# Tables instead of two constant paces for the work beside the RWKV heads

## The chip, the cores and the metric

One core of a Trainium2 chip runs the whole program. The metric is the device time of one execution, in microseconds (us); lower is better. The core's engines run their own instruction streams: PE is TensorE (PEld its weight loads), DVE is VectorE, ACT is ScalarE, POOL is GpSimd, SP is SyncE, which starts the weight transfers.

## The reference, cut to what matters

The program computes three transformer blocks, one after the other. Only the first is touched, and in it two branches that read the same normed input of 528 rows:

```python
o_rwkv = rwkv7_mix(p_rwkv, ...) @ rwkv_w_o[layer]
o_diff = diff_attention(p_diff, ...) @ diff_w_o[layer]
...
def step(S, inp):
    rt, wt, kt, vt, at, bt = inp
    sa = jnp.einsum('bhvk,bhk->bhv', S, at)
    S = S * wt[:, :, None, :] + sa[..., None] * bt[:, :, None, :] + vt[..., None] * kt[:, :, None, :]
    y = jnp.einsum('bhvk,bhk->bhv', S, rt)
    return S, y
```

`rwkv7_mix` has 16 heads of 64 columns, `diff_attention` 8 pairs of heads (causal softmax of two score matrices, their difference times V). Neither needs the other until both are done.

## The kernel before, in words

There is no scheduler: for each engine a Python function writes the instructions in their final order, and each instruction waits for semaphores of the others. In the first block the three functions are `pe_rwkv` (L872), `act_rwkv` (L1133) and `dve_rwkv` (L1269). Each loops over 8 heads here called head 0 to head 7 (each is two RWKV heads, `hh` 0 and 1). The recurrence is computed in 6 chunks of 88 rows (`NCH`, `CH`). One pass of the loop has these parts:

1. transposes of V, At, B and Kh to rows (`rw_tr`), then the products of keys and queries within the chunks (`rw_gram`: ATp, ATo, Ak, Mb, Mk). DVE masks Ak, Mb and Mk, four instructions each (`rw_masked`), and prepares the first inverse (`rw_x`, `rw_xt`, `rw_mask`). Then AV;
2. the inverse of a triangular matrix by doubling: levels 2, 4, 8 and 16, each a product Y and a product Z with small 32x32 matmuls, then 32 and 64 with other shapes;
3. W (`rw_w2`, copied out by ACT as `rw_wt`) and U0 (`rw_u`, copied out by DVE as `rw_u0`);
4. the chain over the chunks, in which chunk ci waits for chunk ci-1: PE multiplies the state by W (`rw_ws`), DVE adds it to U (`rw_us`), PE forms the step of the state (`rw_ds`), DVE adds it to the state (`rw_s`); beside it PE forms the output (`rw_yc`).

Between the parts the function calls `advance()` (L314), at 41 places a head, the same 41 on each engine. They are called place 0 to place 40 here: 0 to 3 in the transposes, 4 to 11 in the products and masks, 12 to 19 in the levels up to 16, 20 to 23 in levels 32 and 64, 24 to 40 in the chain (24 ahead of chunk 0's step of the state, 25 behind it, 26 behind its output, 27 behind `rw_ws` of chunk 1). At a place two kinds of other work may be written into the stream, each cut into steps by `yield`:

- **the work queue** `self.work`: for places 0 to 11 the finish of the head before (`finish`: norm, bonus and output gate), 5 steps; from place 12 on the preparation of the next head (`prep`), 16 steps. On PE its steps 1 to 12 are twelve groups of 12 matmuls of 128x264 (the projections of r, k and v, weights in half slabs), step 13 the matmuls of the decay and of a. On ACT and DVE steps 4, 8 and 12 copy a projection out (`rw_sh`) and mix it with its shifted self (`rw_mixed`, two instructions of DVE of 128x528); step 13 is two sigmoids and three exponentials of ACT and the scan of DVE (`rw_cum`); steps 14, 15 and 16 are DVE's three, four or five wide instructions each, ending with `rw_khat`, for which PE waits ahead of the next head's transposes.
- **the generator** `self.beside` (`pe_diff` L1467, `act_diff` L1566, `dve_diff` L1633): differential attention, 30 steps for each of its 8 heads. Steps 1 to 12 are the projections of q, k and v (on PE 12 matmuls of 128x264 each); 13 transposes V; then for five blocks of queries come the scores (steps 14, 16, 19, 22, 25), on DVE the maximum in the same step and the softmax weights one step later, on PE the transposes of the weights (17, 20, 23, 26, 28) and the product with V (18, 21, 24, 27, 29); step 30 is the norm. The last block's scores (step 25) take four PSUM banks at once.

`advance()` takes one step of the queue, and of the generator 0.7 steps on average:

```python
    def advance(self):

        self.due += self.pace
        while self.due >= 1:
            self.due -= 1
            next(self.beside, None)
        while self.work:
            try:
                next(self.work[0])
                return
            except StopIteration:
                self.work.pop(0)
```

So a head takes 28.7 steps of attention, and which step stands at which place moves from head to head. The preparation of head 0 is written ahead of the loop by `drain()` (L332), with 11 steps of attention beside it at the same pace. Behind the loop, four gate projections (`gate`, L1107) and the finish of head 7 follow, with what is left of the attention.

PSUM has 8 banks, taken in turn (`bank`); whoever takes a bank waits for the instruction that last emptied it. DVE and ACT work strictly in the written order, and a wait of theirs holds up all that stands behind it.

## Time and profile before

| | |
|---|---|
| median of 3 runs | 3495.51 us (3495.16 to 3499.75) |
| profiled execution: its own time, its span | 3494.43 us, 3492.6 us |
| the 8 heads (from the first transpose to the last output) | 107.1 to 1019.2 us of the span |
| PE, DVE, ACT, POOL busy over the span | 88%, 47%, 35%, 24% |
| granted TensorE clock, mean | 0.915 of full speed |

The times of the trace count from the start of the span. In a timeline row the bracket tells how long the engine had been idle before the row and what ended the idle time. TensorE's clock has two levels in the rows, 1.00 (2.4 GHz) and 0.50 (1.2 GHz); a mean between them is a mix over the stretch.

### The profile page before, as it was taken

The page shows a single profiled execution, that of the slowest core. Times are in us where ns is not written, and L with a number is a line of the kernel's source. Part 1 is how long each engine was busy: PE and PEld are TensorE (multiplying, and loading weights), DVE is VectorE, ACT ScalarE, POOL GpSimd, SP SyncE. Part 2 cuts the span into 40 slices and gives each one's busy share as a digit, 9 for nine tenths or more (in the row PEclk, how much of TensorE's full clock was granted, in tenths as well). Part 3 has the DMA queues.
Part 4 walks back from the last instruction along what each step waited for, and adds up shares of the span by engine and source line. Part 5 has one row for each costly group of instructions (what it writes and reads, how often), then busy time and mean ns, then how long its engine had stood idle before and what let it go on. Part 6 is the DMA issues. An engine that isn't in the chain of part 4 may idle for free.

```text
span 3492.6 us, 58593 instructions
## 1 busy us (share of the span) xinstructions
PE 3090.8 (88%) x24118; PEld 2488.9 (71%) x24118; DVE 1644.7 (47%) x2885; ACT 1220.7 (35%) x2083; POOL 831.1 (24%) x808
## 2 busy tenths in 40 slices
PE   6888898889898999999888788888889999888887
PEld 6767787778677878886677566666669998545565
DVE  3544544565524344342454364555565556432432
ACT  2323433433322243233433343433244343332341
POOL 4122121112112100001445355441000002513332
PEclk9888999989869999999899899999999999878998
DMA  3101111111004233331212122214325556301111
GB/s 122 29 28 35 29 41 30 31 32 41 29 25 164 84 121 94 93 97 52 61 55 64 43 64 65 60 58 142 91 78 174 164 164 181 119 20 46 43 46 60
DMA packets 94811, 259.79 MB, mean 74 GB/s; under 512 B 10672, under 2 KB 10672, under 8 KB 93264
## 3 DMA queue, kind: packets, MB, share of 16 engines
q1 hardware_dynamic: 81968, 209.11, 20.3%
q0 software_dynamic: 7680, 35.40, 3.0%
q10 hardware_dynamic: 4896, 11.54, 0.9%
q8 instruction: 191, 3.13, 0.4%
q14 instruction: 76, 0.62, 0.1%
HBM read 236.08 MB, written 19.92 MB: 73 GB/s over the span
## 4 chain that ended last, share of the span: by engine, by line
PE 72%; DVE 13%; ACT 10%; issue 3%; DMA 2%; POOL 1%; ACTq 0%; DVEq 0%; SPq 0%; POOLq 0%
PE psum L430 70%; DVE arena L362 6%; ACT arena L347 5%; ACT arena L355 3%; DVE arena L371 3%; PE psum L434 2%; ACT L343 1%; DMA ring<-in_w 1%; DVE arena L366 1%; ACT L347 1%; DVE arena L383 1%; POOL arena L362 1%; DVE arena L393 0%; DVE arena L386 0%; DMA arena<-in_x 0%
## 5 line engine op out<-in xcount | busy, mean ns | idle before, releaser
L430 PE MATMUL psum<-arena,ring 128*128 128x512 f32 (+3 forms) x6792 | 1640.3, 359 | 19.8 <-DVE arena L362 11.8
L430 PEld LDWEIGHTS psum<-arena,ring 128*128 128x128 f32 (+1 forms) x6792 | 1152.1, 194 | 215.7 <-issue 36.6
L430 PE MATMUL psum<-arena 32*32 32x32 f32 (+10 forms) x12500 | 934.2, 256 | 287.8 <-ACT arena L347 73.6
L430 PEld LDWEIGHTS psum<-arena 32*32 32x32 f32 (+7 forms) x12500 | 653.8, 143 | 525.0 <-issue 202.8
L430 PE MATMUL psum<-arena,arena 128*128 128x512 f32 (+3 forms) x3872 | 987.0, 351 | 32.6 <-DVE arena L362 11.2
L430 PEld LDWEIGHTS psum<-arena,arena 128*128 128x128 f32 (+2 forms) x3872 | 659.7, 188 | 155.6 <-issue 31.6
L355 ACT ACTIVATE arena<-psum 128x512 f32<-128x512 f32 (+14 forms) x660 | 301.5, 457 | 766.4 <-PE psum L430 617.5
L374 POOL CAST ring<-ring 128x512 fp32r<-128x512 f32 x332 | 221.3, 666 | 1208.9 <-DMA ring<-in_w 1199.9
L362 DVE TENSOR_TENSOR arena<-arena 128x528 f32<-128x528 f32 (+9 forms) x638 | 366.8, 575 | 229.8 <-ACT arena L347 123.1
L362 DVE TENSOR_TENSOR ring<-ring,arena 128x1024 fp32r<-128x1024 f32 (+1 forms) x250 | 293.6, 1174 | 338.1 <-ACT arena L355 335.1
L362 POOL TENSOR_TENSOR ring<-ring,ring 128x512 fp32r<-128x512 f32 x332 | 444.4, 1338 | 26.7
L347 ACT ACTIVATE arena<-arena 128x512 f32<-128x512 f32 (+8 forms) x494 | 292.0, 591 | 369.8 <-DVE arena L362 209.5
L355 ACT ACTIVATE arena<-ring 128x1024 fp32r<-128x1024 f32 (+1 forms) x250 | 254.8, 1019 | 462.2 <-PE psum L430 410.9
L362 DVE TENSOR_TENSOR arena<-arena,psum 128x256 f32<-128x256 f32 (+6 forms) x356 | 150.1, 422 | 364.8 <-PE psum L430 353.1
L371 DVE SCALAR_TENSOR_TENSOR arena<-arena 128x512 f32<-128x512 f32 (+8 forms) x237 | 176.8, 746 | 265.6 <-ACT arena L347 255.2
L347 ACT ACTIVATE arena<-psum,arena 128x528 f32<-128x528 f32 (+8 forms) x206 | 117.0, 568 | 256.9 <-DVE arena L383 161.0
L434 PE MATMUL psum<-arena 128*128 128x128 f32 (+2 forms) x693 | 116.1, 306 | 54.0 <-ACT arena L347 16.4
L434 PEld LDWEIGHTS psum<-arena 128*128 128x128 f32 (+2 forms) x693 | 86.9, 148 | 76.5 <-issue 21.8
L371 DVE SCALAR_TENSOR_TENSOR arena<-psum,arena 128x512 f32<-128x512 f32 (+2 forms) x89 | 56.3, 632 | 159.0 <-PE psum L430 141.5
L362 DVE TENSOR_TENSOR arena<-psum,arena 88x264 f32<-88x264 f32 (+2 forms) x149 | 77.5, 520 | 101.3 <-PE psum L430 46.6
L3374 POOL DMA_INDIRECT ring<-in_w,arena_whole x24 | 24.4, 1015 | 390.4 <-PE psum L430 390.4
L347 ACT ACT_TABLE_LOAD x52 | 66.7, 1283 | 125.3 <-PE psum L430 45.3
(51 smaller groups left out, 982.5 us busy)
## 6 DMA issues: line engine op xcount, KB each, us to landing
ring<-in_w SPq DMA_DIRECT2D x202, 512.0 KB, 3.5
ring<-in_w SPq DMA_DIRECT2D x356, 256.0 KB, 2.7
bg<-arena ACTq DMA_DIRECT2D x24, 256.0 KB, 2.1
yd<-arena ACTq DMA_DIRECT2D x10, 512.0 KB, 5.8
arena<-bg POOLq DMA_DIRECT2D x1, 3072.0 KB, 16.7
arena<-in_x SPq DMA_DIRECT2D x1, 2112.0 KB, 14.7
od<-arena POOLq DMA_DIRECT2D x8, 256.0 KB, 2.3
oy<-arena POOLq DMA_DIRECT2D x8, 256.0 KB, 2.3
```

The costliest lines, as they stand in the source:

```text
L343: self.eng.preload_act_table_set("natural_log_exp_and_others")
L347: self.own(self.eng.activation(out, a, f, bias=bias, scale=scale, accum_out=accum), event)
L355: self.own(self.eng.activation(out, a, ACT.Copy, scale=scale), event)
L362: self.own(self.eng.tensor_tensor(out, a, b, op), event)
L366: self.own(self.eng.tensor_scalar(out, a, s1, None, op0), event)
L371: self.own(self.eng.scalar_tensor_tensor(out=out, in0=a, scalar=s, in1=b, op0=op0, op1=op1), event)
L374: self.own(self.eng.tensor_copy(out, a), event)
L383: self.own(self.eng.tensor_reduce(out, a, AXX, op, negate=neg), event)
L430: self.last_ins = self.eng.matmul(out, l, r, start=start, stop=stop, skip_group_check=skip)
L434: self.last_ins = self.eng.transpose(out, a, self.ident[0:n, 0:n])
L3374: G.eng.indirect_dma_start(K.ring[:, slot * SLAB:slot * SLAB + SLAB], None, by_row, bass.IndirectOffsetOnAxis(ap=m.place[:, 4:5], axis=0), ...
```

## The change

`pace` and `due` go. Within the loop over heads, the number of steps at each place comes from two tables of 41 digits, the same for every head and engine: `WORK` for the queue, `BESIDE` for the attention. The sum of `BESIDE` is 30. The preparation of head 0 is written by `begin`, with one step of attention behind each of its first `LEAD` = 9 steps and none behind the other seven. Behind the loop, `place` is `None` and one step of the queue and none of the attention is taken, except in `advance_both`, which now takes one of each.

```diff
-    def advance(self):
-
-        self.due += self.pace
-        while self.due >= 1:
-            self.due -= 1
-            next(self.beside, None)
+    def next_work(self):
...
+    def advance(self):
+
+        work, beside = 1, 0
+        if self.place is not None:
+            n = self.place % len(WORK)
+            work, beside = int(WORK[n]), int(BESIDE[n])
+            self.place += 1
+        for _ in range(beside):
+            next(self.beside, None)
+        for _ in range(work):
+            self.next_work()
+
     def advance_both(self):
-        self.advance()
-        if not self.work:
-            next(self.beside, None)
+        self.next_work()
+        next(self.beside, None)
...
+    def begin(self, beside, lead):
+
+        self.beside = beside
+        while self.work:
+            self.next_work()
+            if lead:
+                lead -= 1
+                next(self.beside, None)
+        self.place = 0
+
+
+WORK = "11121221010111111111121012022101210022001"
+BESIDE = "02010001020201100110101210210211011101011"
+LEAD = 9
...
-    P.beside, P.pace = pe_diff(K, m), 0.7
     P.work.append(prep(0))
-    P.drain()
+    P.begin(pe_diff(K, m), LEAD)
...
```

The same three edits stand in the functions of ACT and DVE. No instruction is added or taken away; the order changes. Attention is at step 9 of 30 at the start of every head, so that step 25 stands at place 23, step 26 at 24, steps 27 and 28 at 26, step 29 at 27, steps 30 and 1 at 29, and steps 2 to 9 at places 30 to 40. Of the preparation, steps 11 and 12 stand at places 21 and 22 (before at 22 and 23), step 13 stays at 24, steps 14 and 15 are both at 25 (before at 25 and 26), 16 at 27 as before.

Two places show it. The first is DVE's stream in head 2 between the copies of level 64 (`64x6x24`) and the scan (the row that ends each piece; it is `rw_cum`'s first instruction, 128x528). The three rows of 128x1, 128x528, 128x528 ahead of the scan are the softmax weights of the last block. Before:

```order
L374 COPY arena<-psum 64x6x24 [waits pe_rw,dve]
L374 COPY arena<-psum 64x6x24 [waits pe_rw,dve_rw]
L383 TENSOR_REDUCE arena<-psum 128x1 [waits pe_df,dve_rw]
L383 TENSOR_REDUCE arena<-psum 128x1 [waits dve_df]
L362 TENSOR_TENSOR arena<-arena 128x528 [waits act_rw,dve_df]
L371 SCALAR_TENSOR_TENSOR arena<-arena 128x528 [waits dve]
L374 COPY arena<-psum 88x384 [waits pe_rw,dve_rw] x2
L380 RECIPROCAL arena<-arena 128x1 [waits act_df,dve_rw]
L380 RECIPROCAL arena<-arena 128x1 [waits act_df,dve]
L362 TENSOR_TENSOR arena<-arena 128x1 [waits dve]
L366 TENSOR_SCALAR arena<-arena 128x528 [waits dve]
L371 SCALAR_TENSOR_TENSOR arena<-arena 128x528 [waits dve]
```

With the change:

```order
L384 TENSOR_TENSOR arena<-arena 128x528 [waits act_rw,dve_df]
L393 SCALAR_TENSOR_TENSOR arena<-arena 128x528 [waits dve]
L396 COPY arena<-psum 64x6x24 [waits pe_rw,dve_rw] x2
L405 TENSOR_REDUCE arena<-psum 128x1 [waits pe_df,dve_rw]
L405 TENSOR_REDUCE arena<-psum 128x1 [waits dve_df]
L396 COPY arena<-psum 88x384 [waits pe_rw,dve_df]
L396 COPY arena<-psum 88x384 [waits pe_rw,dve_rw]
L402 RECIPROCAL arena<-arena 128x1 [waits act_df,dve_rw]
L402 RECIPROCAL arena<-arena 128x1 [waits act_df,dve]
L384 TENSOR_TENSOR arena<-arena 128x1 [waits dve]
L388 TENSOR_SCALAR arena<-arena 128x528 [waits dve]
L393 SCALAR_TENSOR_TENSOR arena<-arena 128x528 [waits dve]
```

The two instructions of 128x528 that mix v (step 12) have moved from between the maxima (`TENSOR_REDUCE`) and the copies of U0 (`88x384`) to ahead of the copies of level 64.

The second is PE's stream in head 2 from chunk 0's step of the state (`64x64`, `rw_ds`) to that of chunk 1. L434 (with the change L456) are the transposes of step 28, and the `128x128` rows that wait for ACT's attention (`act_df`) are step 29. Before:

```order
L430 MATMUL psum<-arena 64x88 x4
L430 MATMUL psum<-arena 128x128 x4
L430 MATMUL psum<-arena 88x64 [waits dve_rw,act_rw]
L430 MATMUL psum<-arena 88x64
L434 MATMUL psum<-arena 16x128 [waits act_rw,dve_df]
L434 MATMUL psum<-arena 128x128 x4
L430 MATMUL psum<-arena 64x64
L430 MATMUL psum<-arena 64x64 [waits dve_rw]
L430 MATMUL psum<-arena 64x64
L430 MATMUL psum<-arena 64x64 [waits dve_rw]
L430 MATMUL psum<-arena 64x88 x6
L430 MATMUL psum<-arena 128x128 [waits act_df]
```

With the change:

```order
L452 MATMUL psum<-arena 64x88 x4
L452 MATMUL psum<-arena 128x128 x4
L456 MATMUL psum<-arena 16x128 [waits act_rw,dve_df]
L456 MATMUL psum<-arena 128x128 x4
L452 MATMUL psum<-arena 88x64 [waits dve_rw,act_rw]
L452 MATMUL psum<-arena 88x64
L452 MATMUL psum<-arena 128x128 [waits act_df]
L452 MATMUL psum<-arena 128x128 x4
L452 MATMUL psum<-arena 64x64
L452 MATMUL psum<-arena 64x64 [waits dve_rw]
L452 MATMUL psum<-arena 64x64
L452 MATMUL psum<-arena 64x64 [waits dve_rw]
```

Step 28 has moved ahead of `rw_ws` of chunk 1 (`88x64`), and step 29 from behind chunk 1's output to ahead of its `rw_ds`.

## Rows read from the trace of the kernel before

**Rows 1.** The page: busy time of PE, and the chain that ended last by engine.

```profile
PE 3090.8 (88%) x24118; PEld 2488.9 (71%) x24118; DVE 1644.7 (47%) x2885; ACT 1220.7 (35%) x2083; POOL 831.1 (24%) x808
...
PE 72%; DVE 13%; ACT 10%; issue 3%; DMA 2%; POOL 1%; ACTq 0%; DVEq 0%; SPq 0%; POOLq 0%
```

**Rows 2.** Windows of heads 1, 2, 4, 7: length, then busy us, PEclk, DMA.

```profile
226.50:340.70 114.20, 100.23 (x1493) 86.62 (x1493) 56.15 (x132) 40.55 (x92) 22.80 (x25) 0.87 0.11 32
340.70:457.10 116.40, 100.37 (x1509) 86.49 (x1509) 59.77 (x135) 41.15 (x93) 23.20 (x25) 0.90 0.11 31
...
572.30:683.20 110.90, 97.51 (x1494) 83.74 (x1493) 57.70 (x132) 40.55 (x92) 22.41 (x25) 0.92 0.11 33
...
913.00:1019.20 106.20, 95.56 (x1354) 79.27 (x1352) 41.71 (x112) 31.84 (x81) 11.56 (x13) 0.70 0.07 22
```

**Rows 3.** Waits of PE in heads 1 to 6 (226.5 to 913): us, times, longest.

```profile
PE psum L430 <- DVE arena L362: 35.6, 27, 5.8
PE psum L430 <- ACT arena L355: 20.2, 17, 3.4
PE psum L430 <- DVE arena L374: 10.6, 5, 3.9
PE psum L430 <- ACT arena L347: 7.4, 7, 2.6
...
```

**Rows 4.** Waits of PE in head 0 (107 to 226.5).

```profile
PE psum L430 <- DVE arena L362: 7.4, 5, 4.7
PE psum L430 <- ACT arena L347: 6.0, 1, 6.0
...
```

**Rows 5.** Waits of PE in head 7 (913 to 1019.2).

```profile
PE psum L430 <- ACT arena L355: 5.3, 6, 1.1
...
```

**Rows 6.** Timeline of PE, head 2, place 23 to place 28.

```profile
414.08 1.70 PE L430 MATMUL psum<-arena,ring 128*128 128x264 f32 x12
...
417.49 2.09 PE L430 MATMUL psum<-arena 88*88 88x64 f32 x24 [0.65 <-ACT arena L355]
...
425.69 0.37 PE L430 MATMUL psum<-arena 64*88 64x64 f32 x4 [2.20 <-DVE arena L374]
425.99 0.98 PE L434 MATMUL psum<-arena 128*16 128x128 f32 x5
...
431.25 5.01 PE L430 MATMUL psum<-arena 88*64 88x64 f32 x32 [3.87 <-DVE arena L362]
```

**Rows 7.** Timeline of DVE, head 2, the same places.

```profile
417.54 0.71 DVE L362 TENSOR_TENSOR arena<-arena 128x528 f32<-128x528 f32 x1 [1.71 <-ACT arena L355]
418.28 0.77 DVE L371 SCALAR_TENSOR_TENSOR arena<-arena 128x528 f32<-128x528 f32 x1
...
423.28 1.26 DVE L386 TENSOR_TENSOR_SCAN arena<-arena 128x528 f32<-128x528 f32 x1 [1.12 <-ACT arena L347]
...
430.98 0.47 DVE L362 TENSOR_TENSOR arena<-arena,psum 88x64 f32<-88x64 f32 x2
```

**Rows 8.** Timeline of ACT, head 2, the three exponentials of step 13.

```profile
426.65 1.99 ACT L347 ACTIVATE arena<-arena 128x528 f32<-128x528 f32 x3
```

**Rows 9.** Timeline of PE ahead of head 0's transposes.

```profile
92.13 3.18 PE L430 MATMUL psum<-arena,ring 128*128 128x264 f32 x24
105.62 2.79 PE L434 MATMUL psum<-arena 128*88 128x128 f32 x12 [10.31 <-DVE arena L362]
```

**Rows 10.** Timeline of PE, head 1, place 11: level 2 waits for DVE.

```profile
253.65 0.85 PE L430 MATMUL psum<-arena 32*32 32x32 f32 x36 [1.41 <-DVE arena L362]
255.22 0.85 PE L430 MATMUL psum<-arena 32*32 32x32 f32 x36 [0.73 <-DVE arena L362]
```

**Rows 11.** Windows at the lower clock: behind head 2's stall, and in head 7.

```profile
426.30:443.40 17.10, 12.62 (x74) 9.73 (x72) 8.67 (x17) 5.67 (x11) 1.43 (x3) 0.50 0.03 10
...
955.40:1019.20 63.80, 55.66 (x593) 43.79 (x583) 20.34 (x66) 18.84 (x56) 0.00 (x0) 0.50 0.01 2
```

**Rows 12.** Timeline of all engines, head 1: a projection step at the lower clock.

```profile
319.96 3.01 PE L430 MATMUL psum<-arena,ring 128*128 128x264 f32 x12
```

More of the change, by code:

```diff
@@ L1106, in pe_rwkv @@
         P.work.append(f)
+    P.place = None
     def gate(g, k):
@@ L1188, in finish @@
         yield
-    A.beside, A.pace = act_diff(K, m), 0.7
     A.work.append(prep(0))
-    A.drain()
+    A.begin(act_diff(K, m), LEAD)
     A_, B_, C_ = slice(0, 32), slice(32, 64), slice(64, CH)
```

12 lines of the change are left out of this document (5 added, 7 removed).

## The prediction

> **What bounds the kernel now.** I read the page first: over the span PE is busy 88% of the time and makes up 72% of the chain that ended last, DVE 13% and ACT 10% [rows 1]. So PE is the engine whose idle time counts, and it has little of it. The second view is a window for each head. Heads 1, 2 and 4 last 114.2, 116.4 and 110.9 us, the last one, which prepares no successor, 106.2 us [rows 2]. They contain nearly the same instructions; the reader should see that the length depends little on where the attention happens to stand. The third view, PE's waits over heads 1 to 6, says how much there is to win: its ten groups add up to 85.2 us, 14.2 us a head of about 114, of which 35.6 and 10.6 us are ended by DVE and 20.2 and 7.4 us by ACT [rows 3]; the six smaller groups add 11.4 us. The groups of head 0 add up to 18.7 us, 7.4 and 6.0 us the largest [rows 4], with 10.3 us more ahead of it [rows 9]. Head 7 has 10.5 us, 5.3 us the largest group [rows 5]. That is 125 us in all, and since the change adds and removes no instruction, its effect is the change of these waits, plus what a different clock makes of the same matmuls.
>
> The timeline then says where the waits are. In head 2 the chain of the chunks holds the largest: 0.65 us ahead of the second U0 product, 2.20 us ahead of `rw_ws` and 3.87 us ahead of `rw_ds` of chunk 1, 6.7 us together [rows 6]. DVE shows why: between the mixing of v (0.71 + 0.77 us) and the addition to U of chunk 1 at 430.98 us it goes through U0, the last softmax, the scan and the steps 14 and 15 [rows 7], and ACT's exponentials (1.99 us) stand in that chain [rows 8]. The mask region is the second: level 2 waits 1.41 + 0.73 us for DVE in head 1 [rows 10]. Every head but the last has both. The rest is spread in pieces of about 1 us.
>
> **The change part by part.** No matmul, copy or transfer is new, so each term below is PE's idle time with the change minus that before.
>
> *The opening.* Before, two projection steps of attention (24 matmuls, 3.18 us) were written behind the decay's matmuls and covered a part of the wait for the first preparation; 10.31 us were left [rows 9]. With `LEAD` = 9 nothing is written there, and two steps fewer are done by then. The chain of ACT and DVE is unchanged, so the wait grows by the cover: **+3.2 us**. Bounds: 0 (the same two steps run earlier and the chain starts no later) to 4.8 us, three steps at 1.6 us.
>
> *The stall of the chunk chain, heads 1 to 6.* Steps 14 and 15 of the preparation still stand ahead of the addition to U in DVE's stream; joining them at place 25 shortens nothing. What shortens it is step 12 at place 22: DVE's two mixing instructions (1.48 us [rows 7]) and the copy of ACT ahead of them leave the stretch between the last block's maxima and the scan. At place 22 PE has the level-64 product, step 24 and the scores (1.5 us each) to do before it needs DVE again, so I cost the moved step at nothing there; without that cover it would cost the same 1.5 us. Beside that, step 28 (0.98 us [rows 6]) now stands ahead of `rw_ws` in the 2.20 us wait, and step 29 in the 3.87 us one; they fill time that had been idle, but they need ACT's copies, which stand behind the exponentials, so I count 0.2 us for them and no more. Head 2's stall of 6.7 us becomes 5.0. My count over the timeline's rows of the same places is 42 us for the six heads, 7 us each, so **-12 us**. Bounds: 0 (the length is set by the two table loads and exponentials of ACT, which do not move) and -24 us (3 us left).
>
> *The masks and level 2.* With the attention at step 9 at the start of every head, all eight heads have the softmax of the first blocks in DVE's stream near the masks, as heads 0, 1 and 2 had, while in heads 5 to 7 projections stood there and the wait was about 1 us. It is about 22 us now over eight heads. The maxima no longer stand between the masks, but the first softmax still stands ahead of the first inverse, and I take 3.4 us a head against head 1's 4.2 (2.1 of it in [rows 10]): 27 us, **+5 us**, of which 4 in heads 1 to 6. Bounds: -5 and +15 us.
>
> *The rest of heads 1 to 6.* Projections now fill places 30 to 40 in every head. In heads 1 and 2, where they did so before, the chain waited 1.2 us behind place 28, in heads 3 to 6 2.6 us on average: **-6 us**. The scores that take four banks stand at one place, 23, where head 2 had them and waited 0.65 us [rows 6], instead of up to 2 us elsewhere: **-2 us**. Bounds for both together: 0 and -12 us.
>
> *Head 0.* It had the same stall, with 10.7 us of its waits there (4.7 of the 7.4 us group and the one of 6.0 us [rows 4]); it becomes 5, and the four-bank scores cost less by 2.5 us: **-8 us**, bounds -12 and -2.
>
> *Head 7.* Attention ends at place 29 and two or three places a chunk have nothing beside the chain; seven projection steps that had been there now run in the earlier heads. Masks +2, levels +2.5, chain +1.5: **+6 us**, bounds 0 and +12.
>
> *The clock.* The stretch of 17.1 us behind head 2's stall is granted 0.50, and so is the one of 63.8 us in head 7 [rows 11]; a projection step takes 3.01 us there [rows 12] against 1.70 [rows 6]. In head 7 PE's activity becomes light some 30 us earlier; the small matmuls lose perhaps 4 us. In heads 3 to 6 two more projection steps a head would run behind the stall at the lower clock, 1.3 us each, of which I count 4 us: **+8 us**, bounds -17 and +15.
>
> A page of the Trainium skill speaks to this term. "TensorE: Matmul & The Clock Gate", Part 1, says that the throttled state is the default and that activity releases it. By that rule a shorter stall would keep the clock up, and the term would be negative; the total would then be that of the second rival below.
>
> Sum: 3.2 - 12 + 4 - 6 - 2 - 8 + 6 + 8 = -6.8 us, the mask term's fifth microsecond being in head 7's. Against the profiled execution's 3494.4 us that is 3487.6. The median of the runs stands 1.1 us above the profiled execution, so **3488 us**, 0.2% below 3495.5. About 0.2% (7 us) is what a measurement of this kernel can tell from no change.
>
> **The rivals.**
>
> *The chains only move* (3495 us). For it: heads 1 and 2 differ by where steps 27 to 29 stand, and both lost about 6.7 us in the stall; the length of six heads of before varies by 5 us whatever stands beside them [rows 2]. Then the stall stays, its -12 goes, and so do half of the opening and of head 7. That the change does not do what it says is part of this: `WORK` moves only four of sixteen preparation steps, by one place each, so most of the table could be empty of effect. Against it: mixing v does leave DVE's stretch.
>
> *The stall breaks and the clock stays up* (3470 us). If the stall falls to about 3 us in pieces, the stretch of 17.1 us at 0.50 [rows 11] may not start. Head 4 had little of it and lasted 5.5 us less than head 2 [rows 2]; with 2.5 us of that to be had in seven heads, 17 us more come off. The page of the skill above is the rule behind it. Against: PE still waits for ACT's exponentials, and a wait there of only 3.4 us, head 1's, the longest of the group that ACT ends [rows 3], had the same slow stretch behind it.
>
> *The softmax in front of level 2* (3505 us, slower). The masks keep DVE busy in this region; with the first softmax always ahead of the inverse, DVE waits for ACT's exponentials with nothing to do, in eight heads and not three. If level 2 then waits as in head 1, or 0.5 us more, the region has 4.7 us a head, 37 us against 22, +15. With a stall that stays at 6.5 us or more (-3 instead of -12) and head 7 and the opening as above, the sum is about +10. It decides from 2 us of wait ahead of level 2 on, together with an unchanged stall. For it: heads 5 and 6 had the region almost free, and lose that. Against: the maxima leave the masks.
>
> **How the numbers follow.** The forecast has 0.45, its own range being 3480 to 3495, about half below 3488.5. The chains only moving has 0.18, the clock rival 0.17, the slower rival 0.20. The range, 3468 to 3504 us, reaches from the clock rival to nearly the slower one and leaves out half of each one's far side. Faster by over 0.2%: half of the forecast (0.23), all of the clock rival (0.17), a little of the unmoved case (0.02): 0.42. Within 0.2%: the other half of the forecast less 0.02 (0.20) and most of the unmoved case (0.15): 0.35. Slower: the slower rival and the edges of the others (0.03): 0.23.
>
> **What would show it.** Right: PE's waits in heads 1 to 6 fall from 85 to about 70 us; ahead of `rw_ws` and `rw_ds` of chunk 1 they are about 5 us in each of heads 0 to 6; the wait ahead of head 0's transposes is 13 to 14 us; all of heads 1 to 6 last the same, 114 to 115 us; head 7 is shorter than 106 us, by 3 to 4 us, since its projections are gone, at a mean clock below 0.70. Wrong: a stall of 6.5 us or more, or one under 3 us with a clock above 0.95 behind it; level 2 waiting over 2.5 us in every head; a new wait of PE at places 22 and 23 for the copies of level 64, behind the moved mixing of v; or waits for converted weights (POOL), which stand in none of the larger groups now.

## The result, and the profile after

| | before | with the change |
|---|---|---|
| median | 3495.34 us | 3447.95 us (3436.78 to 3457.96, 4 runs) |
| profiled execution: its own time, its span | 3494.43, 3492.6 us | 3457.96, 3456.2 us |
| the 8 heads, in the profiled executions | 107.1 to 1019.2 us | 106.7 to 978.5 us |
| granted TensorE clock, mean | 0.915 | 0.919 |

The ratio is 0.9859, 95% interval 0.9836 to 0.9882: faster by 1.4%, where 0.2% had been forecast and the range ended at 3468. Between the two profiled executions lie 36.4 us of span. The heads give 40.3 us, their start 0.4 us, and 4.3 us are lost behind them, where the order is hardly touched.

PE's busy time and the chain, from the page of the kernel after (against [rows 1]):

```profile
PE 3073.2 (89%) x24118; PEld 2482.9 (72%) x24118; DVE 1639.4 (47%) x2885; ACT 1220.6 (35%) x2083; POOL 829.6 (24%) x808
...
PE 73%; DVE 11%; ACT 10%; issue 3%; DMA 2%; POOL 1%; ACTq 0%; DVEq 0%; SPq 0%; POOLq 0%
```

PE is busy 17.6 us less with the same 24118 rows of matmuls. The same matmuls can only have got shorter, or closer together.

The windows of heads 0, 1, 2, 4 and 7 of the kernel after (against [rows 2]; length, then busy us of PE, PEld, DVE, ACT, POOL, PEclk, DMA share, GB/s). The window of head 0 starts 2.7 us ahead of it, the others within 1.1 us of the head's start.

```profile
104.00:213.50 109.50, 97.36 (x1509) 86.25 (x1509) 56.34 (x131) 39.35 (x91) 25.60 (x27) 0.90 0.13 35
213.50:325.10 111.60, 100.77 (x1513) 88.06 (x1512) 58.41 (x135) 40.97 (x93) 24.16 (x26) 0.89 0.12 35
325.10:437.80 112.70, 101.87 (x1522) 89.08 (x1521) 59.48 (x136) 41.16 (x93) 24.74 (x27) 0.89 0.12 34
550.50:663.00 112.50, 101.38 (x1521) 88.63 (x1519) 59.28 (x136) 41.16 (x93) 24.49 (x26) 0.91 0.12 35
885.20:978.50 93.30, 81.36 (x1250) 67.57 (x1248) 38.96 (x108) 30.24 (x78) 6.63 (x8) 0.64 0.04 13
```

Heads 1 to 6 last 111.0 to 112.7 us each, where before they lay between 112.6 and 116.4. Head 0 has lost 13.5 us (119.3 to 105.8) and head 7 11.2 us (104.5 to 93.3). Head 7 also has fewer rows of matmuls now, 1250 against 1354 [rows 2]. The projections that it no longer holds stand in the earlier heads: a window over heads 1 to 6 has 9122 rows of PE against 9017.

The waits of PE in heads 1 to 6 (212.4 to 885.2, against [rows 3]; us in all, times, longest):

```profile
PE psum L452 <- ACT arena L377: 25.4, 12, 3.9
PE psum L452 <- DVE arena L384: 20.3, 18, 1.4
PE psum L452 <- DVE arena L396: 9.9, 6, 1.7
PE psum L456 <- DVE arena L393: 4.8, 6, 0.8
```

The line numbers have moved by 22. The wait for DVE's L384 (before L362) has gone from 35.6 to 20.3 us and has no member over 1.4 us; the one for ACT's copies, L377 (before L355), has grown from 20.2 to 25.4 us. Every group shown counts 6, 12 or 18: every head now waits at the same places for the same work, since the attention starts each head at the same step.

The timeline of PE in head 2, places 23 to 28 (start, us; idle before and what ended it), against [rows 6]:

```profile
397.74 3.19 PE L452 MATMUL psum<-arena 64*128 64x264 f32 x32
401.11 0.71 PE L456 MATMUL psum<-arena 128*16 128x128 f32 x5 [0.18 <-ACT arena L369]
403.48 0.37 PE L452 MATMUL psum<-arena 64*88 64x64 f32 x4 [1.66 <-DVE arena L396]
407.72 6.57 PE L452 MATMUL psum<-arena 16*128 16x128 f32 x34 [3.88 <-ACT arena L377]
413.71 1.68 PE L452 MATMUL psum<-arena,ring 128*128 128x264 f32 x5
```

The stall is still there, 5.7 us against 6.7. It is the product of step 29 that waits now, for ACT's copy of the weights that step 28 transposed, and `rw_ds` comes behind it. ACT shows why that copy is late. Its timeline of the same stretch has the sigmoids at 400.27, a table load, the three exponentials and the copies:

```profile
400.27 1.43 ACT L369 ACTIVATE arena<-psum,arena 128x528 f32<-128x528 f32 x2
403.15 1.28 ACT L365 ACT_TABLE_LOAD   x1 [1.45 <-DVE arena L384]
404.44 1.99 ACT L369 ACTIVATE arena<-arena 128x528 f32<-128x528 f32 x3
406.47 1.20 ACT L377 ACTIVATE arena<-psum 128x128 f32<-128x128 f32 x3
```

Between its two halves, the sigmoids and the exponentials, step 13 waits on ACT for the scan of DVE (1.45 us), and the copies stand behind the whole of it, though PE had transposed their input by about 402 (the row at 401.11).

To see where the time of the heads went, PE's idle time was summed between the boundaries of the 41 places, from PE's rows in both traces; a wait belongs to the place that was written last ahead of it, so that level 2's is in place 11. In heads 1 to 6 together, in us:

| places | 0 to 3 | 4 to 11 (masks, level 2) | 12 to 22 (levels) | 23 to 28 (stall) | 29 to 40 | sum |
|---|---|---|---|---|---|---|
| before | 4.6 | 18.0 | 7.5 | 43.9 | 12.4 | 86.4 |
| after | 0.0 | 25.5 | 2.6 | 35.4 | 2.9 | 66.4 |

With heads 0 and 7 the idle time falls from 116.0 to 89.1 us, 27 us of the 40. The other 13 are busy time of PE (796 to 783 us in the heads), although the heads now hold 24 more rows of matmuls, 11868 against 11844: two projection steps (3.2 us at the full clock) that had stood in the opening. And over the same heads the time spent at the lower clock falls from 247 to 210 us. In the table of the experiments these three numbers of each kernel's profiled execution stand as idle, busy and half clock.

### The profile page after: what moved, and what is told of

Same layout as the page of the kernel before. It is cut to its first block, busy times and chain, and to the rows that moved or that the text cites. A ratio compares the mean times of both kernels' runs of the same rounds, so it can differ in the third digit from the quotient of the medians.

```text
span 3456.2 us, 58588 instructions
## 1 busy us (share of the span) xinstructions
PE 3073.2 (89%) x24118; PEld 2482.9 (72%) x24118; DVE 1639.4 (47%) x2885; ACT 1220.6 (35%) x2083; POOL 829.6 (24%) x808
## 4 chain that ended last, share of the span: by engine, by line
PE 73%; DVE 11%; ACT 10%; issue 3%; DMA 2%; POOL 1%; ACTq 0%; DVEq 0%; SPq 0%; POOLq 0%
PE psum L452 71%; DVE arena L384 5%; ACT arena L369 5%; ACT arena L377 3%; DVE arena L393 3%; PE psum L456 2%; ACT L365 1%; DMA ring<-in_w 1%; DVE arena L388 1%; ACT L369 1%; POOL arena L384 1%; DVE arena L415 0%; DMA arena<-in_x 0%; DVE arena L408 0%; DVE arena L396 0%
## 5 line engine op out<-in xcount | busy, mean ns | idle before, releaser
L452 PE MATMUL psum<-arena,ring 128*128 128x512 f32 (+3 forms) x6792 | 1649.1, 361 | 18.4 <-DVE arena L384 11.8
L452 PE MATMUL psum<-arena 32*32 32x32 f32 (+12 forms) x12500 | 916.4, 256 | 267.0 <-ACT arena L377 69.9
L452 PEld LDWEIGHTS psum<-arena 32*32 32x32 f32 (+9 forms) x12500 | 642.4, 144 | 491.7 <-issue 173.9
L377 ACT ACTIVATE arena<-psum 128x512 f32<-128x512 f32 (+17 forms) x660 | 301.5, 457 | 777.4 <-PE psum L452 602.3
L384 DVE TENSOR_TENSOR arena<-arena 128x528 f32<-128x528 f32 (+9 forms) x638 | 362.1, 568 | 230.6 <-ACT arena L369 141.7
L384 DVE TENSOR_TENSOR ring<-ring,arena 128x1024 fp32r<-128x1024 f32 (+1 forms) x250 | 293.5, 1174 | 338.6 <-ACT arena L377 335.8
L384 POOL TENSOR_TENSOR ring<-ring,ring 128x512 fp32r<-128x512 f32 x332 | 443.6, 1336 | 26.7
L377 ACT ACTIVATE arena<-ring 128x1024 fp32r<-128x1024 f32 (+1 forms) x250 | 254.8, 1019 | 462.7 <-PE psum L452 410.0
L384 DVE TENSOR_TENSOR arena<-arena,psum 128x256 f32<-128x256 f32 (+6 forms) x356 | 150.1, 422 | 336.8 <-PE psum L452 325.5
L456 PE MATMUL psum<-arena 128*128 128x128 f32 (+2 forms) x693 | 110.6, 295 | 56.1 <-DVE arena L393 19.9
L456 PEld LDWEIGHTS psum<-arena 128*128 128x128 f32 (+2 forms) x693 | 83.8, 143 | 78.9 <-DVE arena L393 22.5
L384 DVE TENSOR_TENSOR arena<-psum,arena 88x264 f32<-88x264 f32 (+2 forms) x149 | 77.5, 520 | 113.1 <-PE psum L452 58.6
L388 DVE TENSOR_SCALAR arena<-arena 128x512 f32<-128x512 f32 (+10 forms) x163 | 76.6, 470 | 72.7 <-ACT arena L377 49.9
```

Of the source, the lines that this page charges most:

```text
L377: self.own(self.eng.activation(out, a, ACT.Copy, scale=scale), event)
L384: self.own(self.eng.tensor_tensor(out, a, b, op), event)
L388: self.own(self.eng.tensor_scalar(out, a, s1, None, op0), event)
L452: self.last_ins = self.eng.matmul(out, l, r, start=start, stop=stop, skip_group_check=skip)
L456: self.last_ins = self.eng.transpose(out, a, self.ident[0:n, 0:n])
```

## The experiments

The table collects what was run. Each ratio is to the kernel before, on the same chip and in the same series; the kernel before had medians of 3497 to 3500 us there. The series are e0 to e3, e4 to e7, e8 to e11, e12 to e15, and e16; across series the ratios are the safer comparison. "4–11", "12–22", "23–28" are the idle times of heads 1 to 6 at these places.

| run | median (range) | ratio (95%) | idle | busy | half clock | 4–11 | 12–22 | 23–28 |
|---|---|---|---|---|---|---|---|---|
| e0 the change again | 3442.4 (3435.6–3449.8) | 0.9833 (0.9810–0.9855) | 88 | 782 | 207 | 25.5 | 2.6 | 35.4 |
| e1 `WORK` all ones | 3449.0 (3439.2–3453.3) | 0.9862 (0.9841–0.9883) | 88 | 780 | 199 | 25.5 | 2.1 | 34.4 |
| e2 `BESIDE` even | 3511.6 (3509.4–3520.1) | 1.0038 (1.0022–1.0053) | 119 | 819 | 331 | 37.9 | 14.0 | 39.3 |
| e3 both even | 3506.1 (3499.8–3515.6) | 1.0021 (1.0004–1.0037) | 126 | 799 | 284 | 45.0 | 10.0 | 41.2 |
| e4 opening as before | 3440.1 (3438.7–3444.2) | 0.9845 (0.9822–0.9868) | 89 | 773 | 186 | 25.4 | 3.0 | 35.4 |
| e5 masks even | 3468.3 (3458.8–3472.5) | 0.9915 (0.9886–0.9943) | 103 | 785 | 232 | 37.7 | 3.1 | 33.1 |
| e6 levels even | 3495.6 (3491.3–3503.4) | 0.9997 (0.9983–1.0010) | 108 | 812 | 292 | 25.0 | 19.8 | 34.4 |
| e7 preparation early | 3521.8 (3519.5–3529.8) | 1.0072 (1.0049–1.0096) | 117 | 826 | 345 | 23.6 | 57.9 | 4.5 |
| e8 step 13 split on ACT | 3440.4 (3430.8–3442.1) | 0.9836 (0.9813–0.9859) | 70 | 781 | 192 | 24.9 | 2.1 | 19.0 |
| e9 masks filled | 3432.0 (3424.7–3434.9) | 0.9807 (0.9781–0.9834) | 75 | 771 | 167 | 7.8 | 4.3 | 34.4 |
| e10 e8 and e9 | 3430.6 (3420.3–3431.7) | 0.9807 (0.9784–0.9830) | 54 | 787 | 183 | 8.0 | 4.3 | 16.5 |
| e11 steps 23 to 25 at place 21 | 3514.4 (3509.0–3523.7) | 1.0049 (1.0035–1.0064) | 115 | 817 | 293 | 24.9 | 18.9 | 39.9 |
| e12 matmuls in the stall | 3426.5 (3414.6–3435.0) | 0.9792 (0.9766–0.9818) | 67 | 772 | 109 | 25.5 | 2.6 | 15.9 |
| e13 e9 and e12 | 3418.0 (3410.6–3421.1) | 0.9758 (0.9733–0.9783) | 50 | 788 | 122 | 8.0 | 4.8 | 11.8 |
| e14 e10 again | 3424.6 (3421.6–3431.6) | 0.9790 (0.9764–0.9815) | 52 | 796 | 203 | 7.9 | 4.3 | 15.8 |
| e15 the change again | 3442.4 (3430.0–3452.7) | 0.9842 (0.9815–0.9869) | 89 | 770 | 176 | 25.5 | 2.2 | 35.4 |
| e16 e10, matmuls in both waits | 3413.2 (3403.9–3420.7) | 0.9750 (0.9734–0.9766) | 46 | 786 | 112 | 7.8 | 4.4 | 9.8 |

**e0_change, e1_work_ones, e2_beside_even, e3_both_even: which table does it.** e1 has ones throughout `WORK`, so the preparation stands where it stood before (step 12 back at place 23); e2 spreads the 30 steps of attention evenly, still the same in each head; e3 does both.

```diff
-WORK = "11121221010111111111121012022101210022001"
+WORK = "11111111111111111111111111111111111111111"
```
```diff
-BESIDE = "02010001020201100110101210210211011101011"
+BESIDE = "01101110111011011101110111011011101110111"
```

> The change itself again, for its spread. Its four runs went from 3437 to 3458 us while those of before stay within 6 us. If the spread belongs to the kernel, this run shows it again (a range of 10 us or more around 3448); if it was an accident of one chip, the range is below 6 us. The comparison of the others rests on this one.

> WORK is all ones (one step of the queue at each place, as before), BESIDE stays: preparation steps 11 and 12 go back to places 22 and 23, step 14 stays at 25, step 15 goes to 26. My theory (step 12 out of DVE's stretch between the maxima and the scan shortens the stall by 1.5 us a head): about 10 us slower than the change, 3458 us, the waits ahead of rw_ws and rw_ds of chunk 1 longer by 1.5 us a head. Rival (the attention's places do all of it): within 3 us of the change.

> BESIDE is spread evenly over the 41 places (30 a head, so still the same step at the same place in every head), WORK stays. Theory of the lock (what counts is that every head has the same attention at the same place, start at step 9): within 8 us of the change. Theory of the places (steps 28 and 29 in the stall, projections in the second half of the chain, softmax away from the masks): 20 us or more slower than the change, at 3470 or above, with the difference in the waits of heads 1 to 6.

> Both tables even (WORK all ones, BESIDE spread evenly), LEAD 9: what is left of the change is 30 steps a head instead of 28.7 and the opening. If the lock and the emptier last head are worth the gain, 3455 or below; if the places are, 3480 to 3495, near the kernel before. My prediction's terms for head 0, head 7 and the clock put it at 3490.

e1 can't be told from the change: its median is 6.6 us above e0's in the same series, where 10 had been expected if step 12 counted and under 3 if not, but the executions of either spread over 14 us, and the intervals of the ratios overlap. Its stall is 34.4 us against 35.4. So the moved step 12, to which the prediction gave most of the stall's 12 us, shortens nothing there. e2 and e3 are slower than before (for e3, 3480 to 3495 us had been expected). So it isn't enough that every head has the same step at the same place. The right places do it, and they are in `BESIDE`. The waits of PE in e2, heads 1 to 6, have come back: the two largest groups are 34.3 and 31.4 us, where the change has 25.4 and 20.3:

```profile
PE psum L452 <- ACT arena L377: 34.3, 18, 3.4
PE psum L452 <- DVE arena L384: 31.4, 18, 3.8
```

**e4_lead_even: the opening.** The nine steps spread over the sixteen of `begin` and written ahead of each.

```diff
-            self.next_work()
-            if lead:
-                lead -= 1
+            for _ in range((n + 1) * lead // 16 - n * lead // 16):
                 next(self.beside, None)
+            n += 1
+            self.next_work()
```

> Only the opening changes: the nine steps of attention are spread evenly over the sixteen preparation steps of head 0 and written ahead of each, as the kernel before wrote its eleven. My term for the opening said that LEAD = 9 costs 3.2 us because nothing covers the wait for the first preparation. If so, this version is 3 us faster than the change, and the wait ahead of head 0's transposes falls from 12.4 us to about 9. Rival: the chain starts later by as much, no difference within 2 us.

Its ratio to before, 0.9845, lies between those of the change (0.9833, 0.9842, 0.9859): the opening is worth nothing that shows. The wait ahead of head 0's transposes falls from 12.37 to 2.42 us, by more than the 3 us expected, and yet they start no earlier (at 105.30 us with the change):

```profile
105.71 2.20 PE L457 MATMUL psum<-arena 128*88 128x128 f32 x12 [2.42 <-DVE arena L385]
```

So the projections in the opening neither delay nor hasten the chain of ACT and DVE that head 0 starts with. Two of them fewer leave the start where it was, and are work for the heads instead.

**e5_masks_even, e6_levels_even: which part of `BESIDE`.** In e5 the steps 10 to 17 stand at the places of the even table, in e6 the steps 18 to 25; the rest as in the change.

```diff
-BESIDE = "02010001020201100110101210210211011101011"
+BESIDE = "01101110111001100110101210210211011101011"
```
```diff
-BESIDE = "02010001020201100110101210210211011101011"
+BESIDE = "02010001020211011101110010210211011101011"
```

> Attention steps 10 to 17 stand at the places of the even table (maxima and softmax between the masks again), all others as in the change. The even table cost about 65 us. If the order around the masks carries it, this version is 25 us or more slower than the change (3470), with 12 us more of waits at places 4 to 11 of heads 1 to 6. If the levels and the chain carry it, under 12 us slower.

> Attention steps 18 to 25 stand at the places of the even table, so the scores that take four PSUM banks are at place 21, where PE then waits; all others as in the change. If the bank wait and the half clock that follows it carry the even table's loss, this version is 25 us or more slower than the change (3470), with the half-clock stretches behind place 21 back. If only the waits themselves count, about 11 us slower (3458).

e5 gives back 20 to 26 us (3468 against 3442 to 3448); its idle time at the masks is 12 us higher. e6 gives back all of the gain: 1.00 of before. The waits of PE in e6, heads 1 to 6:

```profile
PE psum L452 <- ACT arena L377: 43.8, 30, 3.9
PE psum L452 <- DVE arena L384: 19.8, 18, 1.4
```

The group for DVE is that of the change; the one for ACT's copies has gone from 12 to 30 waits and from 25.4 to 43.8 us. That is 18 us of idle time. The other 30 us are busy time of PE (783 to 812), with a half clock that lasts 82 us longer. But e6 doesn't say what the change gained there: with 19.8 us of idle time at places 12 to 22 its levels are worse than those of the kernel before, which had 7.5.

**e7_prep_early: does the stall follow the preparation.** Its steps 13 to 16 are written at places 19 to 22.

```diff
-WORK = "11121221010111111111121012022101210022001"
+WORK = "11121221010122121212111100000000000000000"
```

> The preparation is written faster: its sixteen steps at places 12 to 22 instead of 12 to 27, so that its last four steps, the chain of sigmoids, scan and exponentials, are over before the chain of the chunks begins. If that chain standing ahead of the addition to U is what holds PE at places 26 and 27, the 34 us of waits there in heads 1 to 6 fall below 12 us and the kernel is 15 to 30 us faster than the change (3420 to 3433). Rival: the same wait moves to the levels, where PE then lacks cover, and the time is 3440 to 3455.

The stall at places 23 to 28 is gone (4.5 us), and the levels hold it instead, 57.9 us. PE in head 3 at place 20:

```profile
532.55 0.29 PE L452 MATMUL psum<-arena_halved 128*128 128x128 bf16 x2
538.85 1.27 PE L452 MATMUL psum<-arena 32*32 32x32 f32 x24 [6.01 <-ACT arena L377]
541.08 1.30 PE L452 MATMUL psum<-arena 32*32 32x32 f32 x24 [0.96 <-ACT arena L377]
544.79 2.75 PE L452 MATMUL psum<-arena 64*24 64x64 f32 x24 [2.42 <-ACT arena L377]
```

The large wait has gone with the preparation's tail in ACT's and DVE's streams; that it costs more in the levels because PE has more behind it that needs the two is a reading of these rows, not a separate test. This is the longest half clock of all kernels, 345 us, and the slowest time. Neither the 3420 to 3433 us expected nor the rival's 3440 to 3455 came.

**e8_act_split, e9_masks_filled, e10_split_and_filled: taking the two large waits away.** e8 ends step 13 of ACT behind the sigmoids, so that ACT doesn't wait for the scan with everything behind it, and has the exponentials in step 14; three digits of `WORK` follow. e9 moves attention to where level 2 waits. e10 is both.

```diff
         A.act(h2(m.a), out_of(K, 2, T, "rw_as", hp), ACT.Sigmoid, "rw_as", hp, bias=p["a0"][:, hp:hp + 1])
+        yield
         A.wait_ge(*at("rw_cum", hp))
...
         A.act(m.cum, m.cum, ACT.Exp, "rw_exp", hp, scale=-EH)
         yield
-        yield
         yield
...
-WORK = "11121221010111111111121012022101210022001"
+WORK = "11121221010111111111121111022101210022001"
```
```diff
-BESIDE = "02010001020201100110101210210211011101011"
+BESIDE = "00000100101012111111101210210211011101011"
```

> In ACT's preparation the two sigmoids stay in step 13 and the three exponentials, which wait for DVE's scan, go to step 14; WORK puts step 13 at place 23, 14 at 24 and 15 at 25. The chain of sigmoids, scan and exponentials then runs beside W and U0 instead of behind them, and ACT's copy of W does not stand behind a wait for DVE. If the length of that chain after place 24 is what holds PE at places 26 and 27, the 34 us of waits there in heads 1 to 6 fall by 12 us or more and the kernel is 12 to 30 us faster than the change (3442): 3412 to 3430. Rival: the wait moves to place 23, ahead of W, and the time stays within 5 us of 3442.

> The last three projection steps of attention (10 to 12) stand at places 5, 8 and 10, among the masks, and steps 13 to 22 one to three places later, all in the levels. If DVE's softmax in front of level 2 and the missing cover there cause the 25 us of waits at places 4 to 11, these fall below 12 us and the kernel is 10 to 30 us faster than the change: 3412 to 3432. Rival: DVE's masks alone hold PE there, or the softmax delays the levels: 3437 or slower.

> Both edits together. If they act at different places, their gains add, and where half-clock stretches vanish too the sum may be larger: 3390 to 3420. If both only trade one wait for another: 3437 or slower.

e8 takes 16 us out of the stall, with 3.9 us of new waits at place 23 in what is left of it, and its median hardly moves (3440 against 3442 to 3448, where 3412 to 3430 had been expected). Its profiled execution, 3430.8 us, is the fastest of its four, so the trace flatters it. e9 wins 10 to 16 us with about the same idle time removed. The waits of PE in e9, heads 1 to 6, show where: the group for L384 has fallen from 20.3 us to 6.9, and 5.9 us are new, ahead of the transposes at place 1.

```profile
PE psum L452 <- ACT arena L377: 27.6, 18, 3.9
...
PE psum L452 <- DVE arena L384: 6.9, 6, 1.2
PE psum L456 <- DVE arena L384: 5.9, 6, 1.0
```

e10 has the idle time of both (54 us) but not the time of both: 3431 and, repeated as e14, 3425, at most 7 us better than e9; 3390 to 3420 had been expected.

**e11_scores_at_21: the scores of the last blocks two places earlier.** Only steps 23, 24 and 25 move, from places 22 and 23 to 21.

```diff
-BESIDE = "02010001020201100110101210210211011101011"
+BESIDE = "02010001020201100110130010210211011101011"
```

> The change with only attention steps 23, 24 and 25 moved to place 21 (they stood at 22 and 23), so that the scores of the last block ask for four PSUM banks behind level 32's products. The even levels cost 54 us. If the bank wait with its half clock is nearly all of that, this version is 35 us or more slower than the change (3477 or above). If the other moved steps (18 to 22) share it, 10 to 30 us slower.

72 us slower than the change, slower than before. Three steps of thirty, moved by one or two places, cost more than the whole change wins. PE in head 3 at place 21:

```profile
517.22 0.49 PE L456 MATMUL psum<-arena 128*16 128x128 f32 x3 [1.31 <-ACT arena L369]
519.35 4.35 PE L452 MATMUL psum<-arena 16*128 16x128 f32 x18 [1.65 <-ACT arena L377]
523.63 0.40 PE L452 MATMUL psum<-arena_halved 128*128 128x128 bf16 x2
523.79 2.99 PE L452 MATMUL psum<-arena,ring 128*128 128x264 f32 x12
```

The transposes of step 23 wait for the exponentials written just ahead of them, the product of step 24 for the copy of what was just transposed, 3.0 us together. Then the projection step takes 2.99 us where the same one takes 1.7 at the full clock. And DVE waits for the four-bank scores, and then for ACT's part of the softmax, with the copies of level 64 behind both (they start at 535.23 us, and PE waits for them):

```profile
524.13 1.45 DVE L405 TENSOR_REDUCE arena<-psum 128x1 f32<-128x528 f32 x2 [4.76 <-PE psum L452]
529.89 0.71 DVE L393 SCALAR_TENSOR_TENSOR arena<-arena 128x528 f32<-128x528 f32 x1 [4.31 <-ACT arena L369]
```

The place lasts 15.3 us in this head at a mean clock of 0.67, and 87.3 us in the six heads against 36.2 with the change. Idle time explains 24 us (17.6 + 9.8 at places 21 and 23, where the change has 3.2 at places 21 to 24), of which other places give some back; the half clock lasts 83 us longer. Which share the four banks have, beside the two waits of steps 23 and 24, this run doesn't separate.

**e12_keep_warm, e13_filled_warm, e14_both_again, e15_change_again, e16_all_warm: is the half clock a cost of its own.** By then most kernels with more half clock had also more waits. These runs separate the two: e12, e13 and e16 add seven useless matmuls of 128x248 a head (into unused columns), which only fill waits. e12 is the change with seven ahead of step 29's product, e13 is e9 with the same, e16 is e10 with three ahead of the wait for `rw_wt` at place 24 and four ahead of step 28's transposes at place 26. e14 and e15 repeat e10 and the change in the same series.

```diff
         P.did("df_tr", hd, i)
         yield
+        if i == 4:
+            o = 512 * K.book.get(("bank", "rw_y", hd), 0) + 264
+            for j in range(7):
+                P.mm(ps[:, o:o + 248], c["ones"], c["cos"][:, 0:248])
+            P.did("df_warm", hd)
         b = P.bank(1, "df_O", hd, i)
```

e16 has them, in the same form, in two other places:

```diff
         P.keep(by, 2)
+        for j in range(3):
+            P.mm(ps[:, 512 * by + 264:512 * by + 512], c["ones"], c["cos"][:, 0:248])
+        P.did("rw_warm", hp)
         P.wait_ge(*at("rw_wt", hp))
...
+        if i == 4:
+            o = 512 * K.book.get(("bank", "rw_y", hd), 0) + 264
+            for j in range(4):
+                P.mm(ps[:, o:o + 248], c["ones"], c["cos"][:, 0:248])
+            P.did("df_warm", hd)
         P.wait_ge(*at("df_w", hd, i))
```

> The change with seven useless matmuls of 128x248 (fp32, about 3 us at the full clock) per head, written at place 27 ahead of step 29, where PE waits 3.9 us; they go to unused columns of the output's PSUM bank. If the half clock behind this wait follows from PE's being idle and costs time of its own, the stretches at places 27 to 30 go and the kernel is 10 to 30 us faster than the change (3412 to 3432) although it does more work. If only the waits cost, or the matmuls do not keep the clock, the time is that of the change or up to 10 us above (3442 to 3455).

> The same matmuls in e9_masks_filled (3432 us). Clock theory: 10 to 25 us faster than it (3407 to 3422), with under 60 us of half clock in heads 0 to 6, where it had 100. Rival: 3432 to 3445.

> e10_split_and_filled again. Waits of 6 us a head against 11: if they are worth their length, 3415 to 3430 and clearly below the change on the same chip. If the half clock takes the gain back, within 10 us of the change.

> The change again, with more executions. Its eight so far lie between 3436 and 3458. If the executions differ by where the half clock falls, the spread stays 15 us or more and the ratio is 0.983 to 0.986.

> The kernel of e10_split_and_filled (masks filled, ACT's scores split over two steps) with seven useless matmuls a head, of 128x248 float32 each, put ahead of the two waits that are left at places 24 and 26: 3 ahead of the wait for rw_wt and 4 ahead of step 28's transposes. Their results go to unused columns. Clock theory (half clock behind each wait costs time of its own, so matmuls in a wait win although they add work): 5 to 15 us faster than e10 and e14 (3424 to 3431), so 3410 to 3420. Rival (what is left of the waits in e10 is too short for the seven matmuls, which then stand in the way, or the half clock left behind the masks' places stays): same as e14 or slower, 3420 to 3432.

e12 is 16 us faster than the change of its own series, and does more work. PE in its head 2, the stall:

```profile
394.23 3.50 PE L452 MATMUL psum<-arena 64*88 64x64 f32 x18 [1.65 <-DVE arena L396]
398.48 3.83 PE L452 MATMUL psum<-arena 16*128 16x128 f32 x34 [0.75 <-ACT arena L377]
```

The product of step 29 starts 4.25 us behind the start of `rw_ws`, as with the change (403.48 to 407.72). Nothing comes sooner. But PE is active in between, and the 34 rows of matmuls that begin with it take 3.83 us instead of 6.57. The windows of heads 1 to 6 with the change, in e12 and in e16:

```profile
212.40:885.20 672.80, 606.42 (x9122) 530.04 (x9121) 356.16 (x811) 246.94 (x558) 149.40 (x157) 0.91 0.12 35
```
```profile
210.00:859.20 649.20, 601.64 (x9207) 525.33 (x9206) 355.11 (x811) 247.24 (x558) 148.54 (x157) 0.96 0.13 36
```
```profile
209.40:850.10 640.70, 609.84 (x9207) 527.12 (x9206) 360.65 (x811) 246.90 (x558) 146.58 (x156) 0.96 0.13 36
```

With 85 more rows of matmuls e12 takes 24 us less (17 us less than e15's profiled execution, whose six heads take 665.8 us): the granted clock goes from 0.91 to 0.96. The same edit on e9 wins 14 us (e13, in the next series), with 72 us of half clock left in heads 0 to 6 where under 60 had been expected, and seven matmuls in e10's waits win 11 us against e14 (e16, again in the next series). e16, at 3413.2 us, is the fastest of all, 2.5% below before. It beats both kernels, as e9, e10, e12 and e13 do; e9 and e10 do it with no work added.

## Why the prediction was wrong

The sign was given 0.42, the size was wrong five to seven times over: -7 us, measured -36 in the profiled executions and -47 in the medians. (Its own sum plus the 1.1 us to the median is 3488.7 and not 3488, which changes nothing.) Step by step, in us:

| step | predicted | measured |
|---|---|---|
| opening | +3.2 | -0.4 (start of head 0), and +3.2 of its work now in the heads |
| stall, heads 1 to 6 | -12 | -8.5 |
| masks and level 2, heads 1 to 6 | +4 | +7.5 |
| rest of heads 1 to 6 | -8 | -19.0 |
| head 0, idle | -8 | -8.2 |
| head 7, idle (masks included) | +6 | +1.3 |
| clock | +8 | about -17 (busy time -13, with 3.2 more work in it) |
| behind the heads | 0 | +4.3 |

- **What bounds the kernel.** Right: PE, through waits for ACT and DVE. But "since the change adds and removes no instruction, its effect is the change of these waits, plus what a different clock makes" held the two apart, and they aren't apart. Among the runs without added matmuls, the busy time of PE in the heads grows with the half clock: 773 us at 186 (e4), 783 at 210 (the change), 796 at 247 (before), 812 at 292 (e6), 826 at 345 (e7). That is a slope of 53 / 159 = 0.33 us for each us at half clock. e12 lies on it too: 772 us less its eight times seven matmuls (27 us busy in the trace) is 745 us at 109. e10 and e14 lie 15 to 17 us above it, e13 and e16, less their added matmuls, some 10. Most of that goes when only the time is counted in which PE is busy at the half clock, since a wait loses nothing by it: that is 141 us in e9 and 172 us in e10, whose half clock is longer by 16 us only. Over the kernels without added matmuls a line through these counts has 0.41 us for each busy us at half clock, with none further than about 5 us from it.
- **The clock: the step that failed.** It was put at +8, in the belief that projections run behind the stall at the half clock, and that head 7 would lose. It measured about -17, the 13 us of busy time and the 3.2 us of moved projections: 247 to 210 us of half clock (head 0 39 to 19, heads 1 to 6 143 to 123, head 7 64 to 68), which at 0.33 makes 12 of them; the other 5 stay open. In heads 1 to 6, by the same places as the idle time, it fell where the prediction had added 4 us: behind the stall, at places 29 to 40, from 50.5 to 17.7 us, and in the stall from 51.9 to 40.3; at the masks it rose from 10.5 to 15.9 and in the levels from 30.5 to 49.0. The 17.1 us behind head 2's stall were granted 0.50 before, with PE busy for 12.62 of them [rows 11]. With the change the stretch of that length behind it has:

```profile
407.70:424.80 17.10, 16.72 (x123) 14.24 (x123) 6.78 (x17) 2.88 (x5) 6.21 (x7) 0.76 0.12 37
```

PE has more to do there, and the full clock is back before the stretch ends. That the work behind the stall is what brings it back fits these rows; it wasn't tried alone. The stretches at the lower clock were looked at one by one [rows 11]; they weren't counted over all heads. That count is 247 us, 27% of the heads' time, and at 0.33 it is some 80 us of lost time, more than any wait. The Trainium skill's page "TensorE: Matmul & The Clock Gate", Part 1, says that activity releases the throttle. The prediction cited it for the rival that the clock stays up, and e12, e13 and e16 agree with it directly: matmuls without use, put into a wait, win 11 to 16 us. Its estimate of what throttled time costs (in "Terms", the share of pulses withheld, by which it would be 0.5 here) is above the 0.33 measured. A part of the difference is in the traces: of the 210 us at half clock with the change PE idles for 34, and a projection step of 1.70 us [rows 6] grows to 3.01 [rows 12], which is 0.44 of its length and not 0.5.
- **The stall of the chunk chain.** The size was near (-8.5 for -12), the reason wrong. "What shortens it is step 12 at place 22" is refuted by e1, which has step 12 back at 23 and a stall no longer than the change's. What is left of the difference is that steps 26 to 29 stand at the same places of the chain in every head; that wasn't tried alone. Steps 28 and 29 were given 0.2 us. The rest of the stall follows the preparation's tail, as e7 shows, and 16 of its 35 us come from one wait of ACT for DVE's scan inside step 13 (e8).
- **The four-bank scores: a term whose weight wasn't seen.** They had -2 us, "where head 2 had them and waited 0.65 us, instead of up to 2 us elsewhere". The idle time in the levels (places 12 to 22) fell by 4.9. e6 and e11 show how much hangs on the places of steps 18 to 25: spread evenly they cost 53 us, three of them misplaced 72. That is what a bad table loses and not what the change won, since the levels of before had less idle time (7.5 us) than e6's (19.8) and less half clock than the change's. The prediction priced the wait ahead of one instruction in one trace, and not what it does behind it: the other streams held up, and the half clock.
- **The rest of heads 1 to 6.** -6 had been given to the chain behind place 28, and it measured -9.5. Places 0 to 3 (-4.6) were overlooked: their waits ahead of and among the transposes are gone in every head. Levels gave -4.9.
- **The masks.** Right in sign and order of size, and the one real loss of the change. Projections at places 5, 8 and 10 instead take 18 us of it away, and 5.9 come back at place 1 (e9).
- **The opening.** The wait grew by 2 us, as less stood in it, but a longer wait there is no later start (e4). The two steps cost their 3.2 us in the heads, so the size was right by luck.
- **Head 0 and head 7.** Head 0's idle time was right to 0.2 us. It lost 13.5 us and not 8, the rest again at the higher clock. Head 7 was expected to be "shorter than 106 us, by 3 to 4 us" and is 11.2 us shorter than the 104.5 us of the same boundaries; its mean clock, 0.64 in the window, was below 0.70 as said. Its projections moved into heads 1 to 6, whose busy time rose by only 6 us for it (606.4 against 600.1).
- **The rivals.** "The stall breaks and the clock stays up", 3470 us, was nearest, for half the right reason: the clock did rise, with the stall unbroken. "The chains only move" had its premises nearly right, since e1 finds no effect of `WORK` and the stall lost 1 us a head, and its time wrong, since it left out the clock and the waits outside the stall. "The softmax in front of level 2" had its mechanism (+7.5) but not its weight; in e5, where there is more of it, it is worth 20 to 26 us.
- **What would show it.** "PE's waits in heads 1 to 6 fall from 85 to about 70 us": 65, by the same list. "About 5 us" ahead of `rw_ws` and `rw_ds` of chunk 1: 1.66 and 3.88, the second now ahead of step 29. "13 to 14 us" ahead of head 0's transposes: 12.4. "114 to 115 us" for each head: 111 to 113. The waits for converted weights and at places 22 and 23 did not come.

## What to carry to other kernels

When two independent streams are interleaved by hand on engines that work in order, place each step by what stands just behind it in the other engines' streams: a step whose input was written one step ago makes PE wait, and even spreading is no neutral choice. Before pricing such a change, count the time at the lower clock over all repetitions and give it a price from the profiles at hand (here 0.33 us a us, or 0.41 for each us that TensorE is busy in it). And where a wait can't be removed, matmuls without use inside it may pay, if their output has somewhere harmless to go.

## What the runs showed of the hardware

- The half clock behind the waits costs time of its own: from e4 to e7, 159 us more of it went with 53 us more busy time of PE for the same matmuls.
- Some 3 us of useless matmuls a head, in a wait of 4 us, took the clock of six heads from 0.91 to 0.96 and 16 us off the program. This is the run that shows the half clock as a cause, since the other waits stayed as they were.
- The change made the executions spread: 3430.0 to 3452.7 us in e15, 23 us. In its three profiled executions the idle time in the heads is 88 to 89 us each time, but the half clock lasts 176, 207 and 210 us, and the busy time goes with it (770, 782, 783). So idle time is a property of the order, and half clock is partly one of the execution. What decides it in a given execution stays open. The time behind the heads, too, differs by some 13 us among profiled executions (2464.5 us in e15, 2477.7 in the first), without an edit there.
- e8 and e10 removed 16 and 18 us of idle time of the stall, against the change and against e9, and their medians moved by at most 8. In e10's case PE's busy time rose by 16 us against e9. The wait had stood at the half clock: of e9's half clock PE idles for 27 us, of e10's for 12, and it is busy for 31 us more of it, which at 0.41 makes 13 of the 16. So the work moved into the wait ran slowly, and the clock didn't come back sooner. Why it didn't, isn't settled.
